# Second attention of a fused two-block kernel: scores, turns and values in another order among the gates' projections

## Chip, cores and metric

One core of one Trainium2 chip. The metric is the device time of one launch in microseconds, median of several runs.

## What is computed

Two transformer blocks in a row on 256 tokens of width 1024, all in float32. The first block (gated linear attention, an MLP, chunk attention, an MLP) is not touched. The change lies in the mixer of the second block:

```python
proj = xn @ w_in                       # u_pool, q, k, v, iq, ik, iw, gates
mixed = einsum(multiscale_pool(u_pool), pool_w) * pool_scale
y_pool = mixed @ w_pool_proj
q, k, iq, ik = rope_partial(...)       # rotary on the first 16 dims of each head
# sparse attention, 8 heads of 64: an indexer scores every key, the
# 64 best causal keys of each query are kept, softmax over those alone
score = einsum('bqh,bhqk->bqk', w, relu(s));  idx = top_k(score, 64)
p = softmax(q . kg * 64**-0.5);  o = p @ vg
y_attn = o @ w_attn_proj
g = sigmoid(gates)                     # two branches of width 1024
merged = g[:, :, 0] * y_pool + g[:, :, 1] * y_attn
return merged @ w_out
```

After it come an RMS norm, a convolutional feed-forward part (22 blocks) and a final norm.

## The kernel before, in words

Every large product is made of three: each weight chunk of 128x2048 is loaded by SP (L409) into one of three raw buffers, ScalarE casts it into its high part (`split_hi`, L1027) and VectorE takes the low part, raw minus high (`split_lo`, L1445); the activations have high and low parts too. TensorE then runs high times high and high times low for all tiles, then low weights times high activations. A chunk is named by its number j; `project(j, w)` multiplies one chunk by all 256 tokens with 48 matmuls of 256 columns (L421), the first 32 on the high part, the last 16 on the low part, into work bank w % 2 of PSUM (banks 0 and 1). `split_hi(j)` waits until chunk j - 3 is done on TensorE, and the load of chunk j waits until the low part of chunk j - 3 is made. `J_MIX` is 97, so the eight gate projections are chunks 108 to 115, `J_MERGE` is 116 to 119 and `J_OUT2` 120 to 123.

Nothing plans the order: each engine has a hand-written program, and semaphores tie them together. Around the change they are:

- **TensorE** (`tensor_program`, L973 to L1013). After the pooled inputs' projections (chunks 106 and 107) and their turns of the rotary embedding (`rope`, L911, bank 7), it waits for all seven rotations (`roped`, 21) at L982. Then eight rounds h: the scores of head h (`att_scores`, two matmuls at L797 and L798, banks 2 and 3), the gate's projection, in rounds 4 and 5 also half of the pooled branch (`pool_half`), then the values of head h - 1 (`values2`, L812 to L824, banks 6 and 7) and the transposition of head h's softmax (`turn2`, L808, banks 4 and 5). In round 1 `turn2(0)` stands right before `values2(0)`. The last values follow the loop. Then the four merge chunks (pooled branch into banks 2 and 3, attention branch into 4 and 5, twice), then the output projection in chunks 120 to 123, whose sums stand in banks 2 to 5 (`y_of`).
- **ScalarE** (`scalar_program`, L1361 to L1391). In round h: the two exponentials of head h (`att_exp`, L1250), the high part of chunk 110 + h, the gate's copy out of PSUM (L1031), the high part of the pooled branch, the copy of the turned softmax to SBUF (`att_turned`, L1262), and after two heads `out_hi` (L1359). After the loop: four sigmoids (L1383), then the high parts of chunks 118 and 119.
- **VectorE** (`vector_program`, L2071 to L2168). The 64 best scores are found in 32 steps of MAX8 and MATCH_REPLACE8 (`top`, L2051), cut into pieces of 4, 4, 12 and 12 between the rotations of q (3, 4) and k (5, 6) and the low parts of chunks 107 to 109. Then the mask (L2089), which GpSimd makes causal (L2374), and eight rounds: `att_softmax` (L1951: scale and mask from PSUM, maxima, wait for ScalarE's exponentials, reciprocal, scaling), the low part of chunk 110 + h, the trailing means of the pooled branch (h < 4) or its residues (h = 4, 5), and `out_lo` (L2133).

Semaphores of the change: `biased` counts scores taken out of PSUM, `scaled` finished softmaxes, `turned` transpositions, `pt_in` their copies, `pv_done` finished values, `att_out` low parts of the attention's output, `pool_gated` and `att_gated` the products of gates and branches, `merged` the low parts of their sum.

```python
e.wait_ge(pool_gated, 2)      # L1008: before the output projection
e.wait_ge(att_gated, 4)
for i in range(2):
    e.wait_ge(merged, i + 1)
    row_chunk(J_OUT2 + i, 4, act_hi, act_lo, 2 * i, 2, i == 0)
```

Of the kernel before, what the change touches and what calls it, by code (L numbers as in the profile page):

```python
# [22 lines left out]
ATT_H, HD = 16, 64  # L23
# [7 lines left out]
ATT2_H = 8  # L31
# [32 lines left out]
J_MIX, J_MERGE, J_OUT2, J_CONV = 97, 116, 120, 124  # L64
# [45 lines left out]
def build(nc, weights, ada, vecs, x_in, x_rows, ada_rows, ln_rows, final_row, w_gk2, rel_bias, pool_w, rope, pool_count, out):  # L110
    with ExitStack() as ctx:
# [61 lines left out]

        def y_of(at, t, n):

            return ps[:, (0 if at in (0, 2) else 2) + 2 * t + n, :]


        TURN_BANKS = ((6, 7, 4, 5), (6, 7, 2, 3), (6, 7, 4, 5), (6, 7, 2, 3), (6, 7, 2, 3))
        BY_HALF = (1, 3)  # L180

        def turned_tile(at, t, k):
# [181 lines left out]
        def evacuated(w):  # L364

            return bank_free[w % 2], w // 2 + 1
# [52 lines left out]
        def tensor_program(e):  # L419
# [18 lines left out]
            def chunk(j, outs, m_hi, m_lo, nk=KT, wide=256, ready=None):  # L438
                at = products(j, outs, m_hi, m_lo, nk, wide, True, False)
                e.wait_ge(hi_full[j % N_SPLIT], j // N_SPLIT + 1)  # L440
                for n in range(len(outs)):
                    for k in range(nk):
                        o, one, two, _, start = at(n, k)
                        if ready and n == 0:
                            e.wait_ge(*ready(k))
                        mm(o, *one, start=start)
                        mm(o, *two)
                e.wait_ge(lo_full[j % N_SPLIT], j // N_SPLIT + 1)
                for n in range(len(outs)):
                    for k in range(nk):  # L450
                        o, _, _, three, _ = at(n, k)
                        last = mm(o, *three)
                last.then_inc(chunk_done, 1)
# [108 lines left out]
            def y_tiles(first, n):  # L562
                return [(y_acc[:, first + i, :], 2 + (first + i) // 2) for i in range(n)]

            def project(j, w):
                e.wait_ge(*emptied(w))
                chunk(j, work_tiles(w), act_hi, act_lo)
# [222 lines left out]
            def att_scores(n, h, qs, ks):  # L790

                p0 = HD * (h % 2)
                rows, k = slice(p0, p0 + HD), h // 2
                sp = ps[:, 2 + h % 2, 0:3 * P]
                if h >= 2:
                    e.wait_ge(biased, 2 * (n - 1))
                e.matmul(sp[:, 0:P], qs[rows, k, 0:P], ks[rows, k, 0:P], start=True, stop=True, skip_group_check=True)  # L797
                e.matmul(sp[:, P:3 * P], qs[rows, k, P:S], ks[rows, k, :], start=True, stop=True,  # L798
                         skip_group_check=True).then_inc(s_done, 1)
# [12 lines left out]
            def values2(h):  # L812
                n, vs, pt_sb = ATT_H + h, m_v, m_pt
                e.wait_ge(*evacuated(W["mv1"]))
                p0 = HD * (h % 2)
                o = ps[p0:p0 + HD, 6 + h // 2 % 2, 0:S]
                pt = pt_sb[h % len(pt_sb)]
                vh = slice(h * HD, (h + 1) * HD)
                e.wait_ge(pt_in, n + 1)
                if h >= 4:  # L820
                    e.wait_ge(att_out, h // 2 - 1)
                e.matmul(o[:, 0:P], vs[:, 0, vh], pt[:, 0, :], start=True, stop=False, skip_group_check=True)  # L822
                e.matmul(o[:, P:S], vs[:, 0, vh], pt[:, 1, :], start=False, stop=False, skip_group_check=True)  # L823
                e.matmul(o[:, P:S], vs[:, 1, vh], pt[:, 2, :], start=False, stop=True,  # L824
                         skip_group_check=True).then_inc(pv_done, 1)
# [153 lines left out]
            def turn2(h):  # L979
                att_turn(ATT_H + h, h, m_s, (scaled, 2 * h + 2))  # L980

            e.wait_ge(roped, 21)  # L982
            for h in range(ATT2_H):
                att_scores(ATT_H + h, h, m_q, m_k)
                project(J_MIX + 11 + h, W[f"gate{h}"])
                if h in (4, 5):
                    pool_half(h - 4)
                if h:
                    if h == 1:
                        turn2(0)  # L990
                    values2(h - 1)
                    turn2(h)
            values2(ATT2_H - 1)


            for h in range(2):
                if h == 0:
                    e.wait_ge(pt_in, ATT_H + ATT2_H)
                    e.wait_ge(biased, 2 * (ATT_H + ATT2_H))
                else:  # L1000
                    e.wait_ge(pool_gated, 1)
                chunk(J_MERGE + 2 * h, y_tiles(0, 4), m_mix_hi, m_mix_lo, nk=4, wide=512,
                      ready=(lambda k: (mix_lo_in, k + 1)) if h == 0 else None)
                if h:
                    e.wait_ge(att_gated, 2)
                chunk(J_MERGE + 2 * h + 1, y_tiles(4, 4), m_o_hi, m_o_lo, nk=4, wide=512,
                      ready=(lambda k: (att_out, k + 1)) if h == 0 else None)
            e.wait_ge(pool_gated, 2)  # L1008
            e.wait_ge(att_gated, 4)
            for i in range(2):  # L1010
                e.wait_ge(merged, i + 1)
                row_chunk(J_OUT2 + i, 4, act_hi, act_lo, 2 * i, 2, i == 0)
# [6 lines left out]
        def scalar_program(e):  # L1019
# [230 lines left out]
            def att_exp(n, h, s, st):  # L1250
                e.wait_ge(s_max, 2 * n + 1)
                e.activation(s[h % 2][:, 0:P], s[h % 2][:, 0:P], ACT.Exp, bias=st[h % 2][:, 0:1],
                             accum_out=st[h % 2][:, 2:3]).then_inc(s_exp, 1)
                e.wait_ge(s_max, 2 * n + 2)
                e.activation(s[h % 2][:, P:3 * P], s[h % 2][:, P:3 * P], ACT.Exp, bias=st[h % 2][:, 1:2],
                             accum_out=st[h % 2][:, 3:4]).then_inc(s_exp, 1)
# [102 lines left out]
                e.activation(m_o_hi[:, n, :], ps[:, 6 + n % 2, 0:S], ACT.Copy).then_inc(o_hi_in, 1)  # L1359

            for h in range(ATT2_H):  # L1361
                att_exp(ATT_H + h, h, m_s, m_st)
                split_hi(J_MIX + 13 + h)
                evacuate(J_MIX + 11 + h, W[f"gate{h}"], (dev if h < 4 else square)[:, (2 * h) % KT:(2 * h) % KT + 2, :],
                         halves(W[f"gate{h}"]))
                if h in (4, 5):
                    e.wait_ge(pool_mm, h - 3)
                    e.wait_ge(roped, 21)
                    for g in (2 * (h - 4), 2 * (h - 4) + 1):
                        e.activation(m_mix_hi[:, g, :], bank(W[f"pool{h - 4}"])[:, g % 2 * S:(g % 2 + 1) * S], ACT.Copy,  # L1370
                                     scale=v_of("pool_scale", g)).then_inc(mix_hi_in, 1)
                if h:
                    if h == 1:
                        att_turned(ATT_H, 0, m_pt)
                    if h % 2 == 0:
                        out_hi(h // 2 - 1)
                    att_turned(ATT_H + h, h, m_pt)
            out_hi(3)
            for h in range(ATT2_H):
                e.wait_ge(*evacuated(W[f"gate{h}"]))  # L1380
            for m in (dev, square):
                for h in range(2):
                    e.activation(m[:, 4 * h:4 * h + 4, :], m[:, 4 * h:4 * h + 4, :], ACT.Sigmoid).then_inc(sigmoid_in, 1)  # L1383
            for h in range(2):
                split_hi(J_MERGE + 2 * h + 2)
                split_hi(J_MERGE + 2 * h + 3)
                for i in range(2):
                    c = slice(4 * h + 2 * i, 4 * h + 2 * i + 2)
                    e.wait_ge(merge_sum, 2 * h + i + 1)
                    e.wait_ge(chunk_done, J_MERGE)  # L1390
                    e.activation(act_hi[:, c, :], dev[:, c, :], ACT.Copy).then_inc(merge_cast, 1)  # L1391
# [46 lines left out]
        def vector_program(e):  # L1438
# [638 lines left out]
                index_sum(h)  # L2077
            split_lo(J_MIX + 9)
            rope(3, m_q[:, 0:2, :], evacuated(W["mq0"]))
            top(4)  # L2080
            split_lo(J_MIX + 10)
            rope(4, m_q[:, 2:4, :], evacuated(W["mq1"]))
            top(4)
            for n in range(2):
                split_lo(J_MIX + 11 + n)
                rope(5 + n, m_k[:, 2 * n:2 * n + 2, :], evacuated(W[f"mk{n}"]))
                top(12)
            e.wait_ge(top_step, 4 * (TOPK // 8))
            e.tensor_scalar(m_mask[:, :], m_score[:, :], TAKEN / 2, NEG, ALU.is_gt, ALU.mult).then_inc(mask_in, 1)  # L2089

# [44 lines left out]

            for h in range(ATT2_H):
                att_softmax(ATT_H + h, h, m_s, m_st, m_mask[:, 0:P], m_mask[:, P:3 * P], (mask_done, 2))
                split_lo(J_MIX + 13 + h)
                if h < 4:
                    pool_means(h)  # L2140
                if h in (4, 5):
                    pool_residue(h - 4)
                if h and h % 2 == 0:
                    out_lo(h // 2 - 1)
            out_lo(3)


# [398 lines left out]
```

## Time and profile before

| | us |
|---|---|
| median of 3 runs | 1099.0 (1097.58 to 1099.05) |
| the profiled execution's own time | 1096.28 |
| its span in the profile | 1094.6 |
| TensorE busy | 1042.9 (95%) |
| VectorE busy | 804.7 (74%) |
| ScalarE busy | 506.4 (46%) |
| TensorE's mean granted clock | 0.974 of full |

The span is the time between the first and the last instruction in the profile; 1.7 us of the execution's own time lie around it. Times are from the span's start. The second attention and its gates run from about 765 to 842.5, the merge chunks to 865, the output projection after that. A group of matmuls shows its modelled duration; consecutive ones overlap a little, so the distance between the starts of two entries is the surer measure.

### The profile page before, as it was taken

The page shows a single profiled execution, that of the slowest core. Times are in us where ns is not written, and L with a number is a line of the kernel's source. Part 1 is how long each engine was busy: PE and PEld are TensorE (multiplying, and loading weights), DVE is VectorE, ACT ScalarE, POOL GpSimd, SP SyncE. Part 2 cuts the span into 40 slices and gives each one's busy share as a digit, 9 for nine tenths or more (in the row PEclk, how much of TensorE's full clock was granted, in tenths as well). Part 3 has the DMA queues.
Part 4 walks back from the last instruction along what each step waited for, and adds up shares of the span by engine and source line. Part 5 has one row for each costly group of instructions (what it writes and reads, how often), then busy time and mean ns, then how long its engine had stood idle before and what let it go on. Part 6 is the DMA issues. An engine that isn't in the chain of part 4 may idle for free. (4 is left out here: it accounts for less than half of the span.)

```text
span 1094.6 us, 16545 instructions
## 1 busy us (share of the span) xinstructions
PE 1042.9 (95%) x6776; PEld 934.5 (85%) x6776; DVE 804.7 (74%) x1105; ACT 506.4 (46%) x681; POOL 67.8 (6%) x143
## 2 busy tenths in 40 slices
PE   7999989999999999999999998999899989999995
PEld 7987779898898898879898997788798879999995
DVE  3498888989887867568776557668774858777775
ACT  2474434343432766534433334533346455555553
POOL 2001210000000121000000000100000000000000
PEclk9999998999999899999999999899899999999998
DMA  9969766899886474325955453543333435555551
GB/s 342 378 230 325 270 231 246 304 339 339 322 319 226 157 257 145 120 112 180 378 186 193 165 193 131 176 146 125 116 116 116 162 123 173 182 198 184 176 190 59
DMA packets 35051, 227.94 MB, mean 208 GB/s; under 512 B 4096, under 2 KB 4224, under 8 KB 10144
## 3 DMA queue, kind: packets, MB, share of 16 engines
q1 hardware_dynamic: 25232, 167.01, 43.4%
q0 software_dynamic: 9744, 59.87, 14.6%
q8 instruction: 54, 0.88, 0.3%
q14 instruction: 21, 0.17, 0.0%
HBM read 225.82 MB, written 1.05 MB: 207 GB/s over the span
## 5 line engine op out<-in xcount | busy, mean ns | idle before, releaser
L1445 DVE TENSOR_TENSOR weight_lo<-weight_raw,weight_hi 128x2048 fp32r<-128x2048 f32 (+1 forms) x188 | 361.6, 1926 | 106.1 <-ACT weight_hi L1027 105.8
L421 PE MATMUL ps<-act_hi,weight_hi 128*128 128x256 f32 x1336 | 337.0, 290 | 2.7 <-DVE act_lo L1570 2.7
L1027 ACT ACTIVATE weight_hi<-weight_raw 128x2048 fp32r<-128x2048 f32 (+2 forms) x168 | 299.4, 1786 | 78.9 <-PE ps L421 76.7
L421 PE MATMUL ps<-act_lo,weight_hi 128*128 128x256 f32 x1336 | 332.4, 286 | 0.0
L421 PEld LDWEIGHTS ps<-act_hi,weight_hi 128*128 128x128 f32 x1336 | 259.8, 194 | 12.8 <-issue 10.5
L421 PEld LDWEIGHTS ps<-act_lo,weight_hi 128*128 128x128 f32 x1336 | 260.3, 195 | 3.2 <-issue 1.0
L421 PE MATMUL ps<-act_hi,weight_lo 128*128 128x256 f32 x1336 | 182.4, 283 | 0.0
L421 PEld LDWEIGHTS ps<-act_hi,weight_lo 128*128 128x128 f32 x1336 | 169.2, 191 | 0.4
L421 PE MATMUL ps<-weight_hi,mlp_hi 128*128 128x512 f32 x256 | 101.8, 398 | 0.0
L421 PE MATMUL ps<-weight_hi,mlp_lo 128*128 128x512 f32 x256 | 100.9, 394 | 0.0
L1209 ACT ACTIVATE mlp_hi<-mlp_relu 128x512 fp32r<-128x512 f32 x32 | 20.3, 633 | 156.1 <-DVE mlp_relu L1870 148.8
L421 PE MATMUL ps<-weight_lo,mlp_hi 128*128 128x512 f32 x256 | 66.4, 395 | 0.0
L421 PE MATMUL ps<-weight_hi,act_hi 128*128 128x512 f32 x144 | 59.6, 414 | 5.8 <-DVE act_lo L1597 4.2
L421 PE MATMUL ps<-weight_hi,act_lo 128*128 128x512 f32 x144 | 58.1, 404 | 0.0
L421 PEld LDWEIGHTS ps<-weight_lo,mlp_hi 128*128 128x128 f32 x256 | 48.2, 188 | 11.2
L421 PEld LDWEIGHTS ps<-weight_hi,mlp_hi 128*128 128x128 f32 x256 | 48.3, 189 | 10.5 <-issue 0.5
L421 PEld LDWEIGHTS ps<-weight_hi,mlp_lo 128*128 128x128 f32 x256 | 48.2, 188 | 10.4 <-issue 0.5
L1489 DVE SCALAR_TENSOR_TENSOR ada_acc<-ada_raw,c_act,ada_acc 128x2048 f32<-128x2048 f32 x21 | 49.3, 2347 | 0.9 <-DVE ada_acc L1489 0.5
L2262 POOL TENSOR_TENSOR row_root<-row_root,minus_half 128x1 f32<-128x1 f32 x14 | 9.1, 650 | 545.4 <-DVE row_root L1690 316.1
L2249 POOL DMA_DIRECT2D ada_raw<-ada x48 | 25.9, 540 | 273.7 <-DVE ada_acc L1489 127.8
L421 PE MATMUL ps<-weight_lo,act_hi 128*128 128x512 f32 x144 | 40.7, 405 | 0.7 <-DVE weight_lo L1445 0.7
L421 PEld LDWEIGHTS ps<-weight_hi,act_hi 128*128 128x128 f32 x144 | 28.2, 196 | 14.7 <-issue 8.5
(319 smaller groups left out, 1345.9 us busy)
## 6 DMA issues: line engine op xcount, KB each, us to landing
weight_raw<-weights SPq DMA_DIRECT2D x144, 1024.0 KB, 5.0
ada_raw<-ada POOLq DMA_DIRECT2D x48, 1024.0 KB, 6.5
weight_raw<-weights SPq DMA_DIRECT2D x23, 512.0 KB, 3.6
row_g<-ln_rows POOLq DMA_DIRECT2D x4, 512.0 KB, 4.3
row_b<-ln_rows POOLq DMA_DIRECT2D x4, 512.0 KB, 6.6
att_bias<-rel_bias POOLq DMA_DIRECT2D x16, 128.0 KB, 3.1
square<-ada_rows POOLq DMA_DIRECT2D x3, 512.0 KB, 3.9
dev<-x_in SPq DMA_DIRECT2D x1, 1024.0 KB, 5.7
```

The costliest lines, as they stand in the source:

```text
L421: return e.matmul(o, a, b, start=start, stop=False, skip_group_check=True)
L1027: e.activation(weight_hi[h][:, 0:size], weight_raw[r][:, 0:size], ACT.Copy).then_inc(hi_full[h], 1)
L1209: e.activation(hid_hi[m][i % 2][:, :, :], relu_buf[m][i % 2][:, :, :], ACT.Square).then_inc(hid_hi_in, 1)
L1445: ins = e.tensor_tensor(weight_lo[h][:, c], weight_raw[r][:, c], weight_hi[h][:, c].bitcast(F32), ALU.subtract)
L1489: ins = e.scalar_tensor_tensor(out=a, in0=ada_raw[slot][:, :], scalar=c_act[:, k:k + 1], in1=a, op0=ALU.mult, op1=ALU.add)
L2249: e.dma_start(ada_raw[i % N_ADA_RING][:, :], ada[i]).then_inc(ada_full[i % N_ADA_RING], 16)
L2262: e.tensor_tensor(row_root[:, t, at + 1:at + 2], row_root[:, t, at:at + 1], minus_half[:, 0:1], ALU.pow).then_inc(row_pow, 1)
```

## The change

The second attention's work on TensorE is put in another order: the scores run one round ahead of the gates' projections, each turn one round and each value product two rounds behind; the last value product stands between the first two merge chunks. ScalarE and VectorE follow that order; VectorE does the top-64 search in pieces of 6, 6 and 20 with the low part of chunk 109 and the last rotation of k behind the first softmax and the second; the output projection's sums move from banks 2 to 5 to banks 0, 1, 6 and 7, and its waits on the gate products fall away.

```diff
--- before.py
+++ after.py
@@ -173,10 +173,10 @@
 
         def y_of(at, t, n):
 
-            return ps[:, (0 if at in (0, 2) else 2) + 2 * t + n, :]
-
-
-        TURN_BANKS = ((6, 7, 4, 5), (6, 7, 2, 3), (6, 7, 4, 5), (6, 7, 2, 3), (6, 7, 2, 3))
+            return ps[:, ((0, 1, 2, 3), (2, 3, 4, 5), (0, 1, 2, 3), (2, 3, 4, 5), (0, 1, 6, 7), (2, 3, 4, 5))[at][2 * t + n], :]
+
+
+        TURN_BANKS = ((6, 7, 4, 5), (6, 7, 2, 3), (6, 7, 4, 5), (6, 7, 2, 3), (2, 3, 4, 5))
         BY_HALF = (1, 3)
 
         def turned_tile(at, t, k):
@@ -979,23 +979,28 @@
             def turn2(h):
                 att_turn(ATT_H + h, h, m_s, (scaled, 2 * h + 2))
 
-            e.wait_ge(roped, 21)
-            for h in range(ATT2_H):
+            def scores2(h):
+                e.wait_ge(roped, 18 + 3 * (h // 4))
                 att_scores(ATT_H + h, h, m_q, m_k)
+
+            scores2(0)
+            scores2(1)
+            project(J_MIX + 11, W["gate0"])
+            for h in range(1, ATT2_H):
                 project(J_MIX + 11 + h, W[f"gate{h}"])
                 if h in (4, 5):
                     pool_half(h - 4)
-                if h:
-                    if h == 1:
-                        turn2(0)
-                    values2(h - 1)
-                    turn2(h)
-            values2(ATT2_H - 1)
+                if h < ATT2_H - 1:
+                    scores2(h + 1)
+                turn2(h - 1)
+                if h >= 2:
+                    values2(h - 2)
+            turn2(ATT2_H - 1)
+            values2(ATT2_H - 2)
 
 
             for h in range(2):
                 if h == 0:
-                    e.wait_ge(pt_in, ATT_H + ATT2_H)
                     e.wait_ge(biased, 2 * (ATT_H + ATT2_H))
                 else:
                     e.wait_ge(pool_gated, 1)
@@ -1003,10 +1008,12 @@
                       ready=(lambda k: (mix_lo_in, k + 1)) if h == 0 else None)
                 if h:
                     e.wait_ge(att_gated, 2)
+                else:
+                    values2(ATT2_H - 1)
                 chunk(J_MERGE + 2 * h + 1, y_tiles(4, 4), m_o_hi, m_o_lo, nk=4, wide=512,
                       ready=(lambda k: (att_out, k + 1)) if h == 0 else None)
-            e.wait_ge(pool_gated, 2)
-            e.wait_ge(att_gated, 4)
+            e.wait_ge(*evacuated(W["gate6"]))
+            e.wait_ge(*evacuated(W["gate7"]))
             for i in range(2):
                 e.wait_ge(merged, i + 1)
                 row_chunk(J_OUT2 + i, 4, act_hi, act_lo, 2 * i, 2, i == 0)
@@ -1359,8 +1366,8 @@
                 e.activation(m_o_hi[:, n, :], ps[:, 6 + n % 2, 0:S], ACT.Copy).then_inc(o_hi_in, 1)
 
             for h in range(ATT2_H):
+                split_hi(J_MIX + 13 + h)
                 att_exp(ATT_H + h, h, m_s, m_st)
-                split_hi(J_MIX + 13 + h)
                 evacuate(J_MIX + 11 + h, W[f"gate{h}"], (dev if h < 4 else square)[:, (2 * h) % KT:(2 * h) % KT + 2, :],
                          halves(W[f"gate{h}"]))
                 if h in (4, 5):
@@ -1370,17 +1377,16 @@
                         e.activation(m_mix_hi[:, g, :], bank(W[f"pool{h - 4}"])[:, g % 2 * S:(g % 2 + 1) * S], ACT.Copy,
                                      scale=v_of("pool_scale", g)).then_inc(mix_hi_in, 1)
                 if h:
-                    if h == 1:
-                        att_turned(ATT_H, 0, m_pt)
-                    if h % 2 == 0:
-                        out_hi(h // 2 - 1)
-                    att_turned(ATT_H + h, h, m_pt)
-            out_hi(3)
+                    att_turned(ATT_H + h - 1, h - 1, m_pt)
+                if h in (3, 5, 7):
+                    out_hi((h - 3) // 2)
+            att_turned(ATT_H + ATT2_H - 1, ATT2_H - 1, m_pt)
             for h in range(ATT2_H):
                 e.wait_ge(*evacuated(W[f"gate{h}"]))
             for m in (dev, square):
                 for h in range(2):
                     e.activation(m[:, 4 * h:4 * h + 4, :], m[:, 4 * h:4 * h + 4, :], ACT.Sigmoid).then_inc(sigmoid_in, 1)
+            out_hi(3)
             for h in range(2):
                 split_hi(J_MERGE + 2 * h + 2)
                 split_hi(J_MERGE + 2 * h + 3)
@@ -2077,14 +2083,13 @@
                 index_sum(h)
             split_lo(J_MIX + 9)
             rope(3, m_q[:, 0:2, :], evacuated(W["mq0"]))
-            top(4)
+            top(6)
             split_lo(J_MIX + 10)
             rope(4, m_q[:, 2:4, :], evacuated(W["mq1"]))
-            top(4)
-            for n in range(2):
-                split_lo(J_MIX + 11 + n)
-                rope(5 + n, m_k[:, 2 * n:2 * n + 2, :], evacuated(W[f"mk{n}"]))
-                top(12)
+            top(6)
+            split_lo(J_MIX + 11)
+            rope(5, m_k[:, 0:2, :], evacuated(W["mk0"]))
+            top(20)
             e.wait_ge(top_step, 4 * (TOPK // 8))
             e.tensor_scalar(m_mask[:, :], m_score[:, :], TAKEN / 2, NEG, ALU.is_gt, ALU.mult).then_inc(mask_in, 1)
 
@@ -2135,13 +2140,18 @@
 
             for h in range(ATT2_H):
                 att_softmax(ATT_H + h, h, m_s, m_st, m_mask[:, 0:P], m_mask[:, P:3 * P], (mask_done, 2))
+                if h == 0:
+                    split_lo(J_MIX + 12)
+                if h == 1:
+                    rope(6, m_k[:, 2:4, :], evacuated(W["mk1"]))
                 split_lo(J_MIX + 13 + h)
                 if h < 4:
                     pool_means(h)
                 if h in (4, 5):
                     pool_residue(h - 4)
-                if h and h % 2 == 0:
-                    out_lo(h // 2 - 1)
+                if h in (4, 6):
+                    out_lo((h - 4) // 2)
+            out_lo(2)
             out_lo(3)
 
 
```

## Rows read from the trace of the kernel before

**Rows 1.** The page: busy time of each engine

```profile
PE 1042.9 (95%) x6776; PEld 934.5 (85%) x6776; DVE 804.7 (74%) x1105; ACT 506.4 (46%) x681; POOL 67.8 (6%) x143
```

**Rows 2.** Chain that ended last, in order of time: start us, us, what

```profile
789.32 8.37 PE ps L421 x48
797.68 0.36 PE ps L822 x2
...
798.49 0.48 PE ps L808 x3
798.96 0.41 PE ps L797 x2
...
799.81 5.95 PE ps L421 x48
...
841.06 0.63 issue
...
842.53 22.43 PE ps L421 x192
864.96 1.43 issue
```

**Rows 3.** TensorE's timeline: start us, us, operation, count [idle before <- releaser]

```profile
765.01 1.02 PE L916 MATMUL ps<-mix_k,mix_rope 128*128 128x512 f32 x2
768.59 0.48 PE L797 MATMUL ps<-mix_k,mix_q 64*128 64x128 f32 x2 [2.56 <-DVE mix_k L2034]
...
782.10 0.49 PE L808 MATMUL ps<-ident,mix_s 128*128 128x128 f32 x3
785.40 0.66 PE L822 MATMUL ps<-mix_pt,mix_v 128*64 128x128 f32 x2 [2.81 <-ACT mix_pt L1262]
```

**Rows 4.** Stretches: us, busy PE, PEld, DVE, ACT, POOL, PEclk, DMA share, GB/s

```profile
799.85:808.64 8.79, 8.79 (x68) 7.99 (x69) 6.72 (x19) 3.88 (x7) 0.00 (x0) 1.00 0.22 60
765.00:770.00 5.00, 2.44 (x12) 1.28 (x11) 4.96 (x12) 0.60 (x1) 0.00 (x0) 1.00 0.47 147
784.00:785.00 1.00, 0.00 (x0) 0.00 (x0) 0.57 (x1) 1.00 (x3) 0.00 (x0) 0.78 0.00 0
794.00:795.00 1.00, 1.00 (x7) 1.00 (x7) 1.00 (x1) 0.00 (x0) 0.00 (x0) 0.60 0.00 0
893.00:894.00 1.00, 0.52 (x4) 0.55 (x4) 0.69 (x3) 1.00 (x4) 0.00 (x0) 0.90 0.00 0
897.00:898.00 1.00, 1.00 (x10) 1.00 (x9) 0.00 (x0) 1.00 (x1) 0.60 (x1) 0.90 0.00 0
```

**Rows 5.** VectorE's timeline around the mask, and the last low part of the output

```profile
759.46 0.69 DVE L2032 TENSOR_TENSOR mix_rope<-ps,mix_rope 128x512 f32<-128x512 f32 x1 [1.21 <-PE ps L916]
...
764.32 2.28 DVE L1445 TENSOR_TENSOR weight_lo<-weight_raw,weight_hi 128x2048 fp32r<-128x2048 f32 x1
...
768.45 0.61 DVE L2060 MAX8 mix_top<-mix_score 128x8 f32<-128x128 f32 x2
...
772.10 0.36 DVE L2089 TENSOR_SCALAR mix_mask<-mix_score 128x384 f32<-128x384 f32 x1
773.37 0.82 DVE L1959 SCALAR_TENSOR_TENSOR mix_s<-ps,mix_mask 128x128 f32<-128x128 f32 x2 [0.91 <-POOL mix_mask L2374]
...
775.63 0.55 DVE L1968 TENSOR_SCALAR mix_s<-mix_s,mix_st 128x128 f32<-128x128 f32 x2
...
842.98 0.42 DVE L2133 TENSOR_TENSOR mix_o_lo<-ps,mix_o_hi 128x256 fp32r<-128x256 f32 x1 [3.15 <-ACT mix_o_hi L1359]
...
865.00 1.29 DVE L2157 TENSOR_TENSOR square<-square,ps 128x512 f32<-128x512 f32 x2 [1.70 <-PE ps L421]
```

**Rows 6.** ScalarE's timeline: the first turned copy; from the sigmoids' table load to the next weight

```profile
784.78 0.47 ACT L1262 ACTIVATE mix_pt<-ps 128x384 f32<-128x384 f32 x1
...
842.97 1.28 ACT L1383 ACT_TABLE_LOAD   x1
...
848.07 3.69 ACT L1027 ACTIVATE weight_hi<-weight_raw 128x2048 fp32r<-128x2048 f32 x2
```

## The prediction

> **What bounds the kernel now.** I read the page first, then the chain that ended last in order of time, then TensorE's timeline at its gaps, and last the two engines that end these gaps. The page shows TensorE busy for 1042.9 us, 95% of the span, and VectorE for 74% [rows 1]: work taken off VectorE or ScalarE is worth nothing by itself, and what an order can win is TensorE's idle time and its slow clock. The chain through the second attention lies on TensorE from 785.40 to 866.38 but for two short pieces, 0.63 us at 841.06 and 1.43 us at 864.96 [rows 2]. TensorE's timeline adds two gaps ahead of that. At 768.59 it had been idle for 2.56 us, until VectorE's last rotation of k; at 785.40 it had been idle for 2.81 us, until ScalarE's copy of the turned softmax [rows 3], which began only at 784.78 [rows 6], since it is queued behind the second exponential, a high part and the gate's copy. Right there the granted clock fell to half: 0.78 in the stretch from 784 to 785, 0.60 from 794 to 795 [rows 4], so about 10.2 us at 1.2 GHz (0.44 of the first, nine whole, 0.80 of the last). After the first gap it stayed at 1.00.
>
> What a round costs without any wait is in the chain: values 0.81 (797.68 to 798.49), turn 0.48, scores 0.85, projection 5.95, together 8.08 us. The same round at the low clock went from 785.40 [rows 3] to 797.68 [rows 2], 12.28 us; 4.2 us are the clock's.
>
> **The change, part by part.** No instruction is added or taken away; they change places. So I walk through the new order with the durations above.
>
> *First gap.* The scores of heads 0 to 3 need only the first two tiles of k, whose rotation (5) ends 1.34 us after 759.46, at about 760.8 [rows 5]. The last rotation on TensorE starts at 765.01, so scores 0 and 1 can follow it at once. The 2.56 us go. Two search pieces grow from 4 to 6 steps; 12 steps take 3.65 us (768.45 to 772.10), so each is 0.6 us longer, and the wait of 1.21 us for TensorE ahead of rotation 5 shows the slack that takes it up [rows 5]. Nothing for it.
>
> *Is VectorE in time after that?* 20 steps at 0.30 us from 760.8 end at 766.9; mask and GpSimd's pass took 1.27 us (772.10 to 773.37); so the first softmax starts at 768.2 instead of 773.4 and ends 2.81 us later, as in the old one (773.37 to 776.18) [rows 5], at 771.0. Only then comes the low part of chunk 109, 2.2 us, done at 773.2 instead of 766.5. TensorE: scores end at about 767.4, gate 0 at 773.3, and gate 1 asks for the low part after two thirds of its 5.95 us, at 777.3. Slack 4.0 us. The load of chunk 112 waits for this low part and so starts some 6.7 us later, but its high part is now wanted two rounds after. The last rotation comes behind the second softmax and is wanted by scores 4, in round 3. Both are covered by rounds of 8.08 us. In the old round of head 3, the one with the longest means, VectorE was busy 6.72 of 8.79 us [rows 4], waits for ScalarE included in the latter; it fits into TensorE's 8.08. I charge nothing; without that cover the price would be what a round exceeds 8.08 by, at most 0.7 us in two rounds.
>
> *Second gap and the clock.* `turn2(0)` now comes after gate 1 and `values2(0)` after gate 2, a round later than its copy. Each softmax has a whole round more to reach `turn2`, each copy a whole round to reach `values2`. ScalarE's high part of chunk 110 + h moves ahead of the exponential; it needs only the gate before last. The 2.81 us go. With no gap here the clock has no idle time before it to fall after, so I take away the 4.2 us too.
>
> *End of the loop.* The 0.63 us at 841.06 are the last values' wait for the last copy [rows 2]; `values2(6)` and a merge chunk now stand between. They go.
>
> *Merge.* What is late next is here. `values2(7)` stands after chunk 116, and chunk 117 needs `out_lo(3)` at its fourth step. In the old trace `values2(7)` ended at 842.53 [rows 2] and the low part at 843.40 (842.98 + 0.42) [rows 5]: 0.87 us. Chunk 117 has three steps of two matmuls before it, 6 x 0.12 (22.43 / 192) = 0.7 us. A stall of 0.2 us. ScalarE must be free: sigmoids and table load take 5.1 us (842.97 to 848.07) [rows 6]; they start after the last turned copy, some 0.5 us after `turn2(7)`, while TensorE has 0.81 + 5.61 (22.43 / 4) + 0.81 = 7.2 us to do. Slack about 1.6 us. The high parts of chunks 118 and 119 come up to 1.5 us later relative to TensorE, and chunk 118 starts 5.6 us after: hidden. Bounds of this term: 0 (all hidden) to 5.1 (the sigmoids wholly in front of it); I take 0.2, from the rows of the same three instructions.
>
> *Output projection.* Its sums stand in banks that only the gates' copies must have left, so it no longer waits for VectorE's two products, which end at 866.29 (865.00 + 1.29) [rows 5], right before TensorE's resumption at 866.38. The inputs of the first two chunks were merged a merge half earlier. The 1.43 us go [rows 2]. Other banks cost nothing in themselves; bound 0 to 0.3 us either way, from the smallest gaps that the chain shows here (0.63, halved).
>
> Sum: 2.56 + 2.81 + 4.2 + 0.63 + 1.43 - 0.2 = 11.4 us. All that follows is a TensorE-bound stage whose loads and low parts are triggered by TensorE's own progress, so it shifts as a whole. The profiled execution took 1096.28 us (span 1094.6 and 1.7 around it): 1084.9. The median of the runs shown is 2.7 us above this execution; set against it, 1087.6 us.
>
> **A rule weighed.** The rows show a fall of the clock after an idle time of 2.81 us and none after one of 2.56 us [rows 3, 4], so the 4.2 us hang on a narrow difference. The Trainium skill (TensorE: Matmul & The Clock Gate, "What's actually happening") says that the unit that watches TensorE runs freely and "doesn't reset when your kernel starts"; by it the fall is not tied to the gap, and another execution may lack it, or have it at 768 as well. By it the clock term would be anything from 0 to 8.4 us instead of 4.2.
>
> **The rivals.**
>
> *The clock's part isn't won in the median execution* (it was not there, or the fall moves). Then only 11.4 - 4.2 = 7.2 us are left: 1091.8. The next fall, from 893.8 to 897.2, lasts only 3.4 us (0.2 of the first stretch, three whole, 0.2 of the last) [rows 4]; a shifted kernel could have it as long as the 10.2 us of the one before, which costs (10.2 - 3.4) / 2 = 3.4 us: 1091.0. For: the median is 2.7 us above the profiled execution. Against: such luck falls on both kernels alike.
>
> *The merge takes the place of the old waits*: the sigmoids stand in front of `out_hi(3)` by more than their slack. Half of 5.1 us lost: 1090.2. Against: 1.6 us of slack.
>
> *VectorE's backlog*: the low part of chunk 109 more than 4.0 us late. The change would bring nothing only if it came 15 us late, at about 788. Time near 1099. For: VectorE was busy 4.96 of 5 us from 765 to 770 [rows 4]. Against: the search's last 12 steps alone separate old and new.
>
> *Slower: the low clock in the gates' rounds.* If the mixture of small matmuls between two projections, with the first two scores in one lump, let the clock fall for whole rounds, each costs 4.2 us. The idle terms give 7.2, so from three low rounds of eight (one was there before) it is slower; with all eight, 7 x 4.2 - 7.2 = 22 us: 1121. Against: the round at 799.85 to 808.64, with the same mixture, had 1.00 [rows 4].
>
> **How the numbers follow.** Forecast as summed 0.70 (with the case that both gaps had a fall: 4.2 better, 1083.4); clock's part missing or moved 0.14; merge 0.08; backlog or an order that brings nothing 0.04; slower 0.04. The first three are faster by over 0.2% (2.2 us, about what a measurement of this kernel can tell from no change): 0.92; the same 0.04; slower 0.04. The range takes in the forecast with one more fall won (1083.4, to which I give little, so 1084) and the 1091.8 of the missing clock term, with 1 us for a stall in the merge on top: 1084 to 1092.8.
>
> **What would show it.** Right: no idle time of over 0.5 us on TensorE from 765 to 855, clock 1.00 throughout; the mask by 767.5; gate 7 done some 9.5 us earlier than in the trace of before; output projection starting right at chunk 119's end, near 855. The values at the merge: a gap of 0.2 us, ended by `out_lo`. Wrong: TensorE waiting in gate 1 for the low part of chunk 109, or in chunk 117 for more than 1 us, or a clock of 0.50 anywhere in the rounds; or a longer low stretch than 3.4 us in the norm behind the output projection.

## The result, and the profile after

The changed kernel takes 1084.18 us (median of 4 executions, 1083.4 to 1084.37), the kernel before 1098.29 us beside it (4 executions, 1097.24 to 1099.05). The ratio is 0.9871, 95% interval 0.9854 to 0.9888: faster, by 14.1 us. Forecast were 1087.6 us and a range of 1084 to 1092.8; the measured time lies inside, at its lower end. The profiled execution took 1083.4 us, its span 1081.7 against 1094.6.

The page of the changed kernel, its span and busy times, beside [rows 1]:

```profile
span 1081.7 us, 16550 instructions
PE 1034.1 (96%) x6776; PEld 927.0 (86%) x6776; DVE 802.9 (74%) x1105; ACT 506.4 (47%) x681; POOL 67.7 (6%) x143
```

The same work is done. TensorE's busy time falls by 8.8 us although its matmuls are as many. Only 5.3 us of that lie in the part that was changed (93.95 us busy from 765.01 to 866.38 before, 88.67 from 764.78 to 853.48 after): there it is time at the low clock, and matmuls that now run beside each other. The other 3.6 us lie ahead of it, in unchanged code (735.32 against 731.76), and made that part only 0.2 us shorter.

The chain through the stage, in order of time (start us, us, what), beside [rows 2]:

```profile
764.94 0.86 PE ps L916 x2
765.80 0.43 PE ps L797 x4
766.23 0.43 PE ps L798 x4
766.66 11.71 PE ps L421 x96
...
779.22 0.48 PE ps L808 x3
779.70 5.75 PE ps L421 x48
...
786.30 0.48 PE ps L808 x3
786.78 0.36 PE ps L822 x2
...
787.36 0.22 PE ps L824 x2
787.58 5.94 PE ps L421 x48
```

Scores follow the rotation at once, where [rows 3] had 2.56 us of idle time. The first two projections stand in one piece. The first values (L822, at 786.78) follow a turn without a wait, where [rows 3] had 2.81 us; nothing but TensorE's own work follows until the attention's merge chunk.

VectorE's timeline at the mask and at the last low part, beside [rows 5]:

```profile
766.56 0.36 DVE L2094 TENSOR_SCALAR mix_mask<-mix_score 128x384 f32<-128x384 f32 x1
...
770.36 4.49 DVE L1451 TENSOR_TENSOR weight_lo<-weight_raw,weight_hi 128x2048 fp32r<-128x2048 f32 x2
...
836.84 0.42 DVE L2138 TENSOR_TENSOR mix_o_lo<-ps,mix_o_hi 128x256 fp32r<-128x256 f32 x1 [7.31 <-ACT mix_o_hi L1366]
```

TensorE's timeline around that low part, and ScalarE's copy behind the sigmoids, beside [rows 6]:

```profile
837.01 0.28 PE L421 MATMUL ps<-mix_o_lo,weight_hi 128*128 128x256 f32 x1
837.32 0.39 PE L421 MATMUL ps<-mix_o_hi,weight_hi 128*128 128x256 f32 x1
```

```profile
836.43 0.39 ACT L1366 ACTIVATE mix_o_hi<-ps 128x256 fp32r<-128x256 f32 x1 [1.55 <-PE ps L824]
```

The low part of chunk 109 is done at 772.6 (770.36 + 2.2), some 3.8 us before gate 1 wants it (the last third of the 11.71 us piece's second half). At the merge the fourth step starts 0.31 us after the one before instead of 0.12: a stall of 0.19 us. ScalarE had then been free for 1.55 us.

Stretches of the changed kernel, columns as in [rows 4]:

```profile
765.00:855.00 90.00, 89.97 (x697) 82.51 (x696) 64.63 (x134) 48.05 (x76) 0.65 (x2) 1.00 0.40 136
881.00:882.00 1.00, 1.00 (x6) 0.88 (x5) 1.00 (x4) 1.00 (x4) 0.00 (x0) 0.54 0.00 0
884.00:885.00 1.00, 1.00 (x9) 1.00 (x8) 0.00 (x0) 1.00 (x1) 0.60 (x1) 0.76 0.00 0
```

TensorE is busy for 89.97 of 90 us at the full clock. The fall in the norm behind it is there as before, and as long (0.92 of the first stretch, two whole, 0.48 of the last: 3.4 us).

**A measure finer than the medians.** On TensorE all kernels here run the same code up to the last rotation and, but for the banks, from the first matmul of the output projection on. I call the distance between the two starts *the stage*. Before it was 866.38 - 765.01 = 101.37 us; after, the rotation starts at 764.78 and the output projection at 853.48 in TensorE's timeline, 88.70 us. From there to the end it is 228.22 us in both. So the whole difference of the spans (12.9 us) lies in the stage, but for 0.2. In the 14 traces of this study the part ahead of the stage, the same code, took from 764.2 to 767.7 us, and the part behind it from 227.2 to 229.2 us; the low stretches in both differ in place and length. The stage is free of this spread: it is the same to 0.2 us in three traces of the changed kernel. In the kernel before it has a spread of its own, which e9 and e10 below show.

### The profile page after: what moved, and what is told of

It reads as the page before. It is cut to its first block, busy times and chain, and to the rows that moved or that the text cites. A ratio compares the mean times of both kernels' runs of the same rounds, so it can differ in the third digit from the quotient of the medians.

```text
span 1081.7 us, 16550 instructions
## 1 busy us (share of the span) xinstructions
PE 1034.1 (96%) x6776; PEld 927.0 (86%) x6776; DVE 802.9 (74%) x1105; ACT 506.4 (47%) x681; POOL 67.7 (6%) x143
## 4 chain that ended last, share of the span: by engine, by line
PE 84%; DVE 8%; issue 3%; ACT 2%; DMA 2%; POOL 0%; DVEq 0%; POOLq 0%; ACTq 0%
PE ps L421 76%; DVE weight_lo L1451 2%; ACT weight_hi L1034 1%; DMA weight_raw<-weights 1%; PE ps L608 1%; DMA ada_raw<-ada 1%; PE ps L619 1%; PE ps L530 1%; DVE dev L1633 1%; PE ps L808 1%; DVE dev L1626 1%; PE ps L916 1%; DVE att_s L1932 1%; PE ps L798 0%; PE ps L797 0%
## 5 line engine op out<-in xcount | busy, mean ns | idle before, releaser
L421 PEld LDWEIGHTS ps<-act_hi,weight_hi 128*128 128x128 f32 x1336 | 259.4, 194 | 11.4 <-issue 9.0
L2203 DVE SCALAR_TENSOR_TENSOR conv_cv<-ps,vec,conv_cv 128x255 f32<-128x255 f32 x44 | 19.2, 478 | 27.5 <-ACT conv_cv L1419 27.4
```

Source lines behind the costliest of these rows:

```text
L421: return e.matmul(o, a, b, start=start, stop=False, skip_group_check=True)
L2203: steps = [own.of(e.scalar_tensor_tensor(out=cv[p][:, x, 1:S], in0=b[:, x, 0:S - 1], scalar=tap(1, x), in1=cv[p][:, x, 1:S], op0=ALU.mult, ...
```

## The experiments

| kernel | median us | ratio to before (95%) | stage us |
|---|---|---|---|
| before | 1098.29 | | 101.37 |
| before, again (e9) | 1093.69, one execution | | 97.38 |
| before, again (e10) | 1096.65, one execution | | 101.34 |
| before, with filler matmuls (e1) | 1095.0 | 1.0001 (0.9983 to 1.0019) | 97.38 |
| before, new banks (e2) | 1092.9 | 0.9996 (0.9974 to 1.0017) | 97.26 |
| changed, old rounds (e3) | 1086.84 | 0.9915 (0.9891 to 0.994) | 91.35 |
| changed, late start (e5) | 1087.06 | 0.9935 (0.9912 to 0.9958) | 91.52 |
| changed, scores apart (e6) | 1085.4 | 0.9914 (0.9893 to 0.9934) | 89.93 |
| changed | 1084.18 | 0.9871 (0.9854 to 0.9888) | 88.70 |
| changed, again (e4) | 1084.45 | 0.9894 (0.987 to 0.9917) | 88.91 |
| changed, again (e11) | 1085.02 | 0.9924 (0.9902 to 0.9947) | 88.91 |
| scores in pairs (e7) | 1081.23 | 0.9879 (0.9855 to 0.9903) | 85.95 |
| scores and values in pairs (e8) | 1080.26 | 0.9868 (0.9848 to 0.9889) | 84.77 |
| the same, again (e12) | 1081.47 | 0.9891 (0.9867 to 0.9914) | 84.57 |

The kernel before had medians of 1094.01 us (23 executions, 1090.66 to 1100.6) beside e1 to e4, 1094.7 (11) beside e5 to e8 and 1093.6 (11) beside e9 to e12: 3.6 to 4.7 us below the 1098.29 of the first comparison. A stage is read from one traced execution of each kernel.

### Is it the clock, and how much of it?

e1 keeps the second wait of the kernel before and fills it with matmuls:

```diff
                         turn2(0)
+                        for _ in range(12):
+                            e.matmul(ps[:, 7, 0:P], ones_sq[:, :], ident[:, :], start=True, stop=True,
+                                     skip_group_check=True)
```

Expected: 

> The kernel before, with 12 additional matmuls of 128x128 into a free bank between the first turn and the first values, so that TensorE is not idle for the 2.8 us in which it waits for ScalarE's copy. The wait itself stays. Theory (the idle time is what let the clock fall): the granted clock stays at 1.00 from 780 to 797, the time is 4 us below the kernel before, about 1094.3. Rival (the fall comes from something else in the rounds, or costs nothing in most executions): a stretch of 0.50 stays, or the time is within 1 us of the kernel before, 1098.3.

The chain of e1 (L992 are the filler's 12 matmuls; the trace records each of these float32 matmuls twice):

```profile
785.27 2.68 PE ps L992 x24
...
788.09 0.40 PE ps L822 x2
...
790.25 5.94 PE ps L421 x48
```

The wait is still there, 2.82 us, but the projection behind it takes 5.94 us and not 8.37 [rows 2], and the stage is 97.38 us, 4.0 less. With TensorE kept at work the clock does not fall in this trace. Yet over 12 executions the kernel gains nothing (1.0001, and the interval leaves room for 1.9 us at most). The likely reason is that most executions of the kernel before on that chip did not pay those 4 us either; none of the 23 was traced, so this is argued and not shown. Its own further traces, on another chip, show that it can be so.

Expected of e9: 

> The kernel before, once more, for its trace. Theory (two waits on TensorE, one chain behind them, and a clock that may fall after either): from the last rotation to the output projection 97 us where the clock stays up or falls only after the first wait, whose delay the second wait then swallows, up to 101.4 us where it falls after the second; the wait before the first values is 2.8 us less whatever the clock cost before it. Rival (the 101.4 us of the trace shown are what this kernel always takes): 101.4 us within 0.3.

e10: 

> The kernel before a third time, for another trace: same expectations as the one before it.

TensorE's timeline and chain of e9:

```profile
769.04 0.56 PE L797 MATMUL ps<-mix_k,mix_q 64*128 64x128 f32 x2 [2.56 <-DVE mix_k L2034]
...
777.36 0.49 PE L797 MATMUL ps<-mix_k,mix_q 64*128 64x128 f32 x2
...
785.83 0.40 PE L822 MATMUL ps<-mix_pt,mix_v 128*64 128x128 f32 x2 [1.27 <-ACT mix_pt L1262]
```

```profile
788.00 5.95 PE ps L421 x48
```

The stretch in which the clock fell, in e9:

```profile
769.00:770.00 1.00, 0.96 (x4) 0.69 (x4) 1.00 (x6) 0.00 (x0) 0.00 (x0) 0.66 0.81 303
```

And TensorE's timeline and chain of e10:

```profile
785.77 0.66 PE L822 MATMUL ps<-mix_pt,mix_v 128*64 128x128 f32 x2 [2.82 <-ACT mix_pt L1262]
```

```profile
789.70 8.36 PE ps L421 x48
```

The same program has at least two courses. In e10, as in the trace shown first, the clock falls in the second wait, and the stage is 101.3 us. In e9 it fell right after the first wait (0.66 from 769 to 770); head 0's scores and gate 0 took 8.32 us (769.04 to 777.36) instead of 6.80 (768.59 to 775.39 in the trace of before), 1.52 us more. TensorE then came later to the second wait, which had shrunk by the same 1.54 us, from 2.81 to 1.27, and no fall followed. The stage is 97.38 us, as short as with the filler. The expectation is met, its rival is out. In these traces the clock's part of the gain is 0 or 4.0 us, by execution. The Trainium skill (TensorE: Matmul & The Clock Gate, "What's actually happening") says that the unit that sets the clock runs freely and isn't reset at a kernel's start. The traces agree in so far as the wait alone does not decide: after the same 2.56 us the clock stayed up in two of three traces of this program and fell in one.

### The banks of the output projection

```diff
-            return ps[:, (0 if at in (0, 2) else 2) + 2 * t + n, :]
+            return ps[:, ((0, 1, 2, 3), (2, 3, 4, 5), (0, 1, 2, 3), (2, 3, 4, 5), (0, 1, 6, 7), (2, 3, 4, 5))[at][2 * t + n], :]
...
-            e.wait_ge(pool_gated, 2)
-            e.wait_ge(att_gated, 4)
+            e.wait_ge(*evacuated(W["gate6"]))
+            e.wait_ge(*evacuated(W["gate7"]))
```

Expected: 

> The kernel before, with the output projection's sums alone moved to banks 0, 1, 6 and 7 and its waits for the gate products taken away. Theory: the wait of 1.43 us before it goes and nothing else, 1096.9. Rival (the next stage is bound by VectorE's low parts and takes the gain back): 1098.3, with the distance from the first output matmul to the end longer by 1.4 us.

The chain of e2, and TensorE's timeline at the second wait and at the start of the output projection:

```profile
788.08 7.39 PE ps L421 x48
...
838.84 0.63 issue
...
840.31 25.81 PE ps L421 x206
```

```profile
785.89 0.40 PE L822 MATMUL ps<-mix_pt,mix_v 128*64 128x128 f32 x2 [1.31 <-ACT mix_pt L1262]
...
862.78 0.39 PE L421 MATMUL ps<-weight_hi,act_hi 128*128 128x512 f32 x1
```

The stretch in which the clock fell for the second time:

```profile
787.00:788.00 1.00, 1.00 (x6) 0.52 (x4) 0.97 (x5) 0.49 (x1) 0.00 (x0) 0.96 0.00 0
```

The merge chunks run into the output projection without a break (840.31 + 22.4 = 862.7), where [rows 2] had 1.43 us between them; the 0.63 us ahead of the merge stayed. From the first output matmul to the end it is 228.12 us, so nothing is given back. The median can't show it: 0.9996 with 0.2% to either side, and 1.43 us are 0.13%. This trace had a fall behind the first wait and a second one behind the second wait, which was 1.31 us long; its stage of 97.26 us is, to 0.13 us, the 97.38 us of e9, less 1.43, plus 1.44 for the second fall (7.39 us for the projection behind it instead of 5.95). The second fall began 2.0 us after TensorE had gone back to work (785.89, and 0.96 in the stretch from 787 to 788). The 12 executions of e2 lie in two groups, seven from 1090.55 to 1092.97 us and five from 1096.37 to 1099.21, with nothing between; that fits two courses some 4 us apart, but only one of them was traced.

### One part undone at a time

e3 gives the rounds the order of before on all three engines and keeps the early start:

```diff
+            for h in range(ATT2_H):
+                scores2(h)
+                project(J_MIX + 11 + h, W[f"gate{h}"])
+                if h in (4, 5):
+                    pool_half(h - 4)
+                if h:
+                    if h == 1:
+                        turn2(0)
+                    values2(h - 1)
+                    turn2(h)
+            values2(ATT2_H - 1)
```

Expected: 

> The changed kernel, with the eight rounds in the order of before on TensorE, ScalarE and VectorE (values one round behind, the last ones before the merge, exponentials before the high part), but with the early rotation, the long last piece of the search and the new banks. Theory: the second gap of 2.8 us and the 0.6 us before the merge are back, and 0.8 us of the two scores in one lump are lost: 4.3 us above the changed kernel, and 4.2 more if the clock falls after the gap, 1088.5 to 1092.7. Rival (the order of the rounds gives little, the early start gives most): under 1087.

e5 keeps the new rounds and gives rotations and search the order of before:

```diff
-                e.wait_ge(roped, 18 + 3 * (h // 4))
+                e.wait_ge(roped, 21)
...
+            for n in range(2):
+                split_lo(J_MIX + 11 + n)
+                rope(5 + n, m_k[:, 2 * n:2 * n + 2, :], evacuated(W[f"mk{n}"]))
+                top(12)
```

Expected: 

> The changed kernel, with the rotations of k, the search and the low part of chunk 109 in the order of before (pieces of 4, 4, 12 and 12, all rotations before the first scores). Theory: TensorE again waits 2.6 to 2.9 us before the first scores, all else stays: 1086.9, and up to 4.2 us more if the clock falls after it. Rival (the start is covered elsewhere, for instance because VectorE's work behind the mask was the bound): within 1 us of 1084.2.

TensorE's timeline of e3 and VectorE's mask in it, then TensorE's timeline of e5:

```profile
767.80 0.49 PE L797 MATMUL ps<-mix_k,mix_q 64*128 64x128 f32 x2
...
782.78 0.40 PE L822 MATMUL ps<-mix_pt,mix_v 128*64 128x128 f32 x2 [0.99 <-ACT mix_pt L1265]
```

```profile
768.63 0.36 DVE L2091 TENSOR_SCALAR mix_mask<-mix_score 128x384 f32<-128x384 f32 x1
```

```profile
768.37 0.50 PE L797 MATMUL ps<-mix_k,mix_q 64*128 64x128 f32 x4 [2.55 <-DVE mix_k L2040]
```

e5 is as expected: the first wait is back, 2.7 us (91.52 - 88.84, the mean of the changed kernel's three traces), and no second one.

e3 misses: I had put 4.3 to 8.5 us on the old rounds, and they cost 2.5 in the stage, and 2.4 in the medians; 1086.84 us lies in the rival's "under 1087". The second wait came back as 0.99 us only, without a fall of the clock; with the 0.63 us ahead of the merge, 0.85 for the two scores and 0.38 for two projections (both explained under e6), less the 0.19 us stall, this makes 2.7.

With the early start the mask comes 0.83 us behind the first scores (768.63 against 767.80) and not 3.51 (772.10 against 768.59), so the second softmax, ScalarE's exponentials and the first copy, which the old rounds wait for, come earlier against the scores too. The early start alone takes 1.8 of the 2.81 us of the second wait, the new rounds alone all of it: from the kernel before with new banks (99.94 us if its clock falls) the early start alone saves 8.6 us, the new rounds alone 8.4, both together 11.1. Counted from the course without the late fall (97.38 - 1.43 = 95.95 us) it is 4.6, 4.4 and 7.1 us. Parts that end the same wait don't add. Nor does the early start "give most", as e3's rival has it: the two parts weigh the same.

### What two heads' scores cost

```diff
             scores2(0)
-            scores2(1)
             project(J_MIX + 11, W["gate0"])
+            scores2(1)
```

Expected: 

> The changed kernel, with the scores of head 1 behind gate 0's projection, where they were before, and no longer right behind those of head 0. Theory (two heads' scores stand on the two halves of the array's rows and run beside each other when nothing stands between them: 0.87 us for both in the trace of after, 0.85 for each in that of before): 0.85 us more in the stage, 1085.0. Rival (only the place changes, each costs what it costs): no difference, 1084.2.

The chain of e6:

```profile
766.35 0.41 PE ps L797 x2
766.76 0.43 PE ps L798 x2
767.20 5.95 PE ps L421 x48
773.15 0.42 PE ps L797 x2
773.56 0.43 PE ps L798 x2
774.00 5.94 PE ps L421 x48
```

Apart, each head's scores take 0.85 us; in one lump both take 0.86 (765.80 to 766.66 above): four matmuls in 0.43 us, where apart two take 0.41. The stage is 1.1 us longer, 0.85 of it for this. The other 0.2 us are in the projections: behind scores or values one takes 5.94 or 5.95 us, behind a turn or another projection 5.75. The Trainium skill (TensorEngine Tiling (Array Packing), "Key Properties") says that tiles on separate parts of the array load and multiply in parallel and that a change of the tiling drains TensorE. The trace agrees with the first: heads 0 and 1 stand on rows 0 to 63 and 64 to 127 (their matmuls are shown as 64*128). It fits the second: 0.19 us is what a projection pays behind another shape; that a drain is the reason no run here shows.

### Versions beyond the change

e7 pairs the other scores, e8 (and e12) the values too:

```diff
-                if h < ATT2_H - 1:
-                    scores2(h + 1)
+                if h in (1, 3, 5):
+                    scores2(h + 1)
+                    scores2(h + 2)
                 turn2(h - 1)
-                if h >= 2:
-                    values2(h - 2)
+                if h in (3, 5, 7):
+                    values2(h - 3)
+                    values2(h - 2)
```

Expected of e7: 

> The changed kernel, with the scores of heads 2 and 3, 4 and 5, 6 and 7 in lumps too, behind gates 1, 3 and 5. Theory of the overlap: three times 0.85 us less, 1081.7. Rival (the second of each pair needs VectorE to have read the bank two heads before, and waits for it): 1084.2 or above, with idle time on TensorE at L797 ended by VectorE.

of e8: 

> As the one before, and with the values of heads 0 and 1, 2 and 3, 4 and 5 in lumps as well, behind gates 3, 5 and 7. Their outputs stand on different halves of the array's columns. If column halves run beside each other as row halves do, 0.8 us less for each of the three pairs, 1079.3; if not, as e7, 1081.7.

of e11: 

> The changed kernel beside the kernel of paired scores and values on one chip: 1084.3; 88.7 to 88.9 us in the stage, the same in each trace, since nothing in it lets the clock fall.

of e12: 

> Paired scores and paired values again, beside the changed kernel. Theory: 84.8 us in the stage, 4.1 us under the changed kernel, ratio to the kernel before 0.985. Rival (the difference between the two was one of chips and runs): within 1 us of the changed kernel.

The chain of e7 behind gate 3, then that of e8 at the same place:

```profile
793.36 0.43 PE ps L797 x4
793.79 0.43 PE ps L798 x4
```

```profile
791.76 0.41 PE ps L797 x2
792.18 0.43 PE ps L798 x2
792.61 0.08 issue
792.69 0.46 PE ps L797 x2
793.15 0.43 PE ps L798 x2
793.58 0.48 PE ps L808 x3
794.06 0.36 PE ps L822 x2
...
795.13 5.95 PE ps L421 x48
```

VectorE in e8, as it takes head 3's scores out of the bank that head 5's go into:

```profile
791.92 0.62 DVE L1967 SCALAR_TENSOR_TENSOR mix_s<-ps,mix_mask 128x128 f32<-128x128 f32 x2
```

e7: 2.9 us off the stage (85.95), 2.55 forecast; the rest is projections that no longer stand behind scores. Two heads' values in one lump take 1.07 us (794.06 to 795.13) against 2 x 0.81: column halves run beside each other only in part, 0.55 us less for a pair and not 0.8. The stage is 84.6 to 84.8 us, 1.2 to 1.4 less than e7 and not 2.4.

The three pairs give 1.65, and three projections that no longer stand behind values 0.57; but 0.96 is lost again behind gate 3. There the scores of heads 4 and 5 take 1.82 us (791.76 to 793.58) and not 0.86: the second head's start only when VectorE has taken head 3's scores out of their bank (791.92 + 0.62 = 792.54, the scores at 792.69). That is the wait that the rival of e7 named. It did not come in e7, where TensorE reaches this lump 1.0 us later behind the rotation and it takes 0.86 us, and came in both traces of the paired values (e12: 1.84 us).

On one chip the paired kernel took 1081.47 us (1080.7 to 1082.34) and the changed kernel 1085.02 (1083.17 to 1086.42): 3.6 us less, in line with the 4.3 us between their stages there. It is the fastest version here and beats both kernels; its ratio to the kernel before, 0.9891, missed the 0.985 expected: the kernel before stood at 1093.6 us there. e4 and e11 confirm the stage of the changed kernel to 0.2 us, with the clock at 1.00 throughout; from there to the end they took 228.9 us and not the 228.2 expected of e4.

Expected of e4: 

> The changed kernel again, beside the others on one chip. Both theories: 1084.2, ratio 0.987; from the first rotation of k's second half to the first matmul of the output projection 88.7 us, and 228.2 us from there to the end.

## Why the prediction was right, and where it was off

Time and sign are right, and the time lies in the range, 0.2 us above its lower end. By its steps, for the two traces shown first (12.67 us in the stage, 11.4 forecast):

- *First gap*: 2.56 forecast; scores now start 0.95 us after the rotation and did so 3.58 us after it: 2.63. Right.
- *VectorE in time*: mask at 766.56 and low part of chunk 109 at 772.6, forecast 766.9 and 773.2. Right; the rival of VectorE's backlog did not come.
- *Second gap and the clock*: 2.81 and 4.2 (4.0 by the two courses) are gone, and the clock stood at 1.00. Right for these traces. What failed is the step that takes the 4.2 us as the kernel's: they are paid in one course of the kernel before (101.3 us) and not in the other (97.4). The rule that was weighed beside the sum had said so; the chance of 0.14 for it was too low. Beside e4 and e11, on one chip each, the kernel before had 1094.01 and 1093.6 us and the changed kernel 1084.45 and 1085.02: 9.6 and 8.6 us less (11.6 and 8.3 by the ratios), where the stages say 12.5 with the late fall and 8.5 without. So between 2.5 and 5.8 of the 14.1 us of the first comparison depend on the executions in which the kernel before was measured. That the time came out right is in part luck: 1087.6 is a gain of 11.4 us taken from a median of 1099.0. The changed kernel took 1084.2 to 1085.0 us everywhere; taken from the 1094 us of the other chips, the same sum would have given 1082.6.
- *Also off in that step*: I named only the later values and turns as what ends the second wait. e3 shows that the early start alone leaves 0.99 us of it.
- *End of the loop and output projection*: 0.63 and 1.43 us went; e2 shows the second by itself. Right.
- *Merge*: 0.2 us forecast, 0.19 measured, by the same three instructions. ScalarE's slack was 1.55 us, forecast 1.6. The rival of the sigmoids is out.
- *A term that was missing*: "So I walk through the new order with the durations above" priced the two first scores at 0.85 us each. In one lump they cost 0.86 together: 0.84 us more gain. And two projections no longer stand behind another tile shape: 2 x 0.19. These 1.2 us are the difference between 11.4 and 12.67. With every term as measured (2.63 + 2.81 + 4.0 + 0.63 + 1.43 - 0.19 + 1.2) the sum is 12.5, and 0.15 us stay open.
- *Gate 7 done 9.5 us earlier* was forecast, as a sign; it ended at 827.5 against 839.8, 12.3 us earlier. I left out that one head's values (0.81) and turn (0.48) now stand behind it, and the 1.2 us above.
- The 3.4 us between 1087.6 and 1084.18 are these 1.2, 0.2 ahead of the stage, and for the rest the executions: I carried over that the median of before stood 2.7 us above its profiled execution, and the changed kernel's stands 0.8 us above its own.
- *Slower by a low clock in the rounds*: 1.00 in all traces with the new rounds. Out.

## What to carry to other kernels

A gap on the bound engine has to be followed back to the whole chain that ends it: two edits may each remove the same wait, and then their gains don't add. A clock that falls after a wait is a gain only in the executions that had the fall; look at more than one trace, and measure the stretch between two unchanged instructions rather than the whole kernel. Put small matmuls that use different halves of the array's rows next to each other, and look whether the second has to wait for its bank: in e8 that cost 0.96 us.

## What was not expected of the hardware

- Scores of two heads on the two row halves: 0.86 us together, 0.85 us for one. Values on two column halves: 1.07 us together, 0.81 for one.
- 48 projection matmuls take 5.94 us behind matmuls of another tile shape and 5.75 us behind one of the same.
- After one and the same idle time of 2.56 us the clock stayed at 2.4 GHz in two traces of a program and went to 1.2 GHz in a third; that cost 1.5 us, which the next wait gave back in full. In e2 it went down after an idle time of 1.31 us and 2.0 us of work.
- In the trace of before TensorE worked on without a pause from 785.40, and the clock came back only at 794.8, 9.4 us later.
